# The mixes of odd heads on GpSimd in two passes, in the first prompt attention of a two-layer decoder step

## The reference

```python
s = jnp.einsum('bqhgcd,bkhcd->bhgcqk', q, k).astype(jnp.float32) * A_DH ** -0.5
...
p = jax.nn.softmax(jnp.where(mask, s + bias, -jnp.inf), axis=-1)
a = p[:, :, :, 0] - lam * p[:, :, :, 1]
o = jnp.einsum('bhgqk,bkhe->bqhge', a.astype(v.dtype), v)
```

## Time and profile before

| | us |
|---|---|
| median of 3 runs | 2816.69 |
| lowest and highest of them | 2816.53, 2825.95 |
| the profiled execution | 2817.39 |
| its span | 2815.7 |
| mean granted TensorE clock, share of full speed | 0.87 |

### The profile page before, as it was taken

How to read it: one execution, slowest core, us unless ns; L and a number is a source line. 1 busy time by engine, 2 the same in 40 slices (tenths; PEclk the granted TensorE clock), 3 DMA queues, 4 the chain that set the end, 5 groups by cost and what they waited for, 6 DMA issues and landing times. The chain is left out here.

```text
span 2815.7 us, 31305 instructions
## 1 busy us (share of the span) xinstructions
PE 2248.9 (80%) x9850; PEld 1356.4 (48%) x9850; DVE 1215.9 (43%) x2588; ACT 667.6 (24%) x1475; POOL 264.3 (9%) x410
## 2 busy tenths in 40 slices
PE   7999997986777775588845699975999938884688
PEld 3454565545676764356622344631654416661333
DVE  1000002675656553499821011064989946630111
ACT  2121001221222220366610011042012116640011
POOL 0000000002323220000013100031000000002300
PEclk9999999997887875699966799997999969986689
DMA  6001111100000002200029800111200120006841
GB/s 231 31 33 45 60 31 33 33 0 15 4 7 4 4 8 60 67 19 16 8 67 306 299 30 23 38 40 63 85 11 34 45 94 24 23 3 206 271 151 42
DMA packets 133268, 180.34 MB, mean 64 GB/s; under 512 B 23104, under 2 KB 103392, under 8 KB 132112
## 3 DMA queue, kind: packets, MB, share of 16 engines
q1 hardware_dynamic: 98648, 130.30, 13.9%
q10 hardware_dynamic: 24640, 25.41, 2.8%
q0 software_dynamic: 9856, 23.13, 2.5%
HBM read 152.48 MB, written 30.70 MB: 65 GB/s over the span
## 5 line engine op out<-in xcount | busy, mean ns | idle before, releaser
L538 PE MATMUL banks<-actT 128*128 128x350 f32 (+1 forms) x960 | 285.4, 461 | 12.3 <-ACTq L548 12.3
L198 PE MATMUL banks<-fr_w,actT 128*128 128x512 f32 (+1 forms) x640 | 238.9, 531 | 0.0
L538 PEld LDWEIGHTS banks<-actT 128*128 128x128 f32 x960 | 183.7, 192 | 113.1 <-ACTq L548 12.5
L474 PE MATMUL banks<-ptg_w,heads 128*128 128x512 f32 (+1 forms) x432 | 185.8, 592 | 1.7 <-ACT heads L426 1.7
L2726 DVE TENSOR_SCALAR_CACHE_REDUCE ch_hits<-c_chosen,ch_cand 128x384 bf16<-128x384 f32 (+1 forms) x186 | 175.8, 945 | 18.0 <-DVE ch_cand L2731 12.2
L198 PEld LDWEIGHTS banks<-fr_w,actT 128*128 128x128 f32 x640 | 113.8, 193 | 126.0 <-issue 126.0
L2170 PE MATMUL banks<-a_pages,actT 128*128 128x512 f32 x384 | 166.3, 593 | 0.0
L474 PEld LDWEIGHTS banks<-ptg_w,heads 128*128 128x128 f32 (+1 forms) x432 | 77.7, 180 | 109.3 <-issue 109.3
L600 PE MATMUL banks<-actT,aq_w 128*128 128x350 f32 (+1 forms) x384 | 120.1, 473 | 12.6 <-DMA aq_w<-w_in_e_dram 12.6
L1546 ACT ACTIVATE aa_prob<-aa_prob,aa_mx 128x128 f32<-128x128 f32 (+7 forms) x128 | 98.1, 767 | 74.0 <-DVE aa_mx L1647 73.7
L2170 PEld LDWEIGHTS banks<-a_pages,actT 128*128 128x128 f32 x384 | 72.3, 190 | 88.9 <-issue 88.9
(11 more groups left out here) (505 smaller groups left out, 3644.3 us busy)
## 6 DMA issues: line engine op xcount, KB each, us to landing
tok_rows<-fr_stage SPq DMA_DIRECT2D x8, 1028.0 KB, 3.9
fr_w<-w_in_e_dram SPq DMA_DIRECT2D x8, 1024.0 KB, 21.1
actT<-w_in_e_dram SPq DMA_DIRECT2D x6, 1024.0 KB, 5.3
a_pages<-cache_a_k_dram SPq DMA_DIRECT2D x48, 128.0 KB, 4.3
a_pages<-cache_a_v_dram SPq DMA_DIRECT2D x48, 128.0 KB, 4.0
a_pages<-w_out_e_dram SPq DMA_DIRECT2D x3, 2048.0 KB, 12.6
ptg_w<-w_in_o_dram SPq DMA_DIRECT2D x3, 2048.0 KB, 12.8
c_pages<-cache_c_k_dram SPq DMA_DIRECT2D x48, 128.0 KB, 3.9
```

Source lines behind the costliest of these rows:

```text
L198: last = nc.tensor.matmul(m.ps[:, j, 0:g[1]], m.actT[:, c, t * P:t * P + P], weights[j][:, c, :], start=(c == 0), stop=(c == KC - 1))
L474: last = nc.tensor.matmul(m.ps[0:r, j, 0:g[1]], rows[:, slot, c, 0:r], weights[j][:, c, :], start=(c == 0), stop=(c == KC - 1))
L538: last = nc.tensor.matmul(m.ps[:, NS * j + k, 0:tn], wring[:, s, c, j * P:(j + 1) * P], m.actT[:, c, t0:t0 + tn], start=(c == 0), stop=(c ...
```

## The change

For odd n the mix moves from DVE to POOL. POOL has no single instruction here for e0 + r e1, so it makes two: a TENSOR_SCALAR product of e1 with r into `mix`, and a TENSOR_TENSOR sum of `mix` and e0, in place. Between the two stands a wait on a new semaphore `mix_step`. The semaphore `combined` becomes `combined0` (signalled by DVE for even heads) and `combined1` (signalled by POOL for odd heads). DVE still computes reciprocal and ratio for all heads. The waits of `maxima` and of the transposes go to the semaphore of their parity. In POOL's program the new stage `mixed` has lag 1 and stands before `root`.

```diff
--- before.py
+++ after.py
@@ -1367,7 +1367,7 @@
             equal, rank = sb("equal", [P, wmax]), sb("rank", [P, wmax])
             neg, count, left = sb("neg", [P, 1]), sb("count", [P, len(tiles)]), sb("left", [P, len(tiles)])
         names = ("neg_set restored mark_step marked written bias_in bias_mm bias_out gate_in gain_in gain_out scores_mm near_out far_out lowest exp_half "
-                 "combined turned probs_out pv_mm o_out rs_out y_ready y_mm y_turned half_set step gated recip_out "
+                 "combined0 combined1 mix_step turned probs_out pv_mm o_out rs_out y_ready y_mm y_turned half_set step gated recip_out "
                  "ratio_out")
         s = {x: m.sem(f"{tag}_{x}") for x in names.split()}
 
@@ -1456,8 +1456,23 @@
                     pool.wait_ge(s["rs_out"], 2 * p.t + 1)
                     nc.gpsimd.tensor_tensor(rs[0:p.R], rs[0:p.R], minus_half[0:p.R], ALU.pow).then_inc(s["rs_out"], 1)
 
+                def mixed(n):
+
+                    p, h = heads[n]
+                    if n % 2 == 0:
+                        return
+                    out = mix[0:p.R, n % 2, 0:p.W]
+                    pool.wait_ge(s["ratio_out"], n + 1)
+                    if n >= 2:
+                        pool.wait_ge(s["turned"], groups_before[n - 1])
+                    nc.gpsimd.tensor_scalar(out, prob[0:p.R, n % 2, 1, 0:p.W], ratio[0:p.R, n % 2:n % 2 + 1], None,
+                                            ALU.mult).then_inc(s["mix_step"], 1)
+                    pool.wait_ge(s["mix_step"], n // 2 + 1)
+                    nc.gpsimd.tensor_tensor(out, out, prob[0:p.R, n % 2, 0, 0:p.W], ALU.add)\
+                        .then_inc(s["combined1"], 1)
+
                 if diff:
-                    pipeline(0, N, [(at_tile_end(root), TURN + 4)])
+                    pipeline(0, N, [(mixed, 1), (at_tile_end(root), TURN + 4)])
 
             @block.tensor
             def _(pe):
@@ -1492,7 +1507,7 @@
                 def turn(n, ks):
                     p, h = heads[n]
                     src = mix[:, n % 2] if diff else prob[:, n % 2, 0]
-                    pe.wait_ge(s["combined"] if diff else s["exp_half"], n + 1)
+                    pe.wait_ge(s[f"combined{n % 2}"] if diff else s["exp_half"], n // 2 + 1 if diff else n + 1)
                     for k in ks:
                         b0, bn = p.groups[k]
                         used = groups_before[n] + k + 1 - len(p.turns)
@@ -1612,7 +1627,7 @@
                     out = lambda c, w0, w1: prob[0:p.R, n % 2, c, w0:w1]
                     bias_p = bias[0:p.R, h, at:at + p.W - near]
                     if n >= 2 and diff:
-                        dve.wait_ge(s["combined"], n - 1)
+                        dve.wait_ge(s[f"combined{n % 2}"], n // 2)
                     elif n >= 2:
                         dve.wait_ge(s["turned"], groups_before[n - 1])
                     if not diff and p.t >= 2:
@@ -1662,12 +1677,14 @@
                     nc.vector.scalar_tensor_tensor(out=r, in0=inv[0:p.R, n % 4, 1:2], scalar=m.lam[0:p.R, 0:1],
                                                    in1=den[0:p.R, n % 4, 0:1], op0=ALU.mult, op1=ALU.mult)\
                         .then_inc(s["ratio_out"], 1)
+                    if n % 2:
+                        return
                     dve.wait_ge(s["ratio_out"], n + 1)
                     if n >= 2:
                         dve.wait_ge(s["turned"], groups_before[n - 1])
                     nc.vector.scalar_tensor_tensor(out=mix[0:p.R, n % 2, 0:p.W], in0=prob[0:p.R, n % 2, 1, 0:p.W],
                                                    scalar=r, in1=prob[0:p.R, n % 2, 0, 0:p.W], op0=ALU.mult,
-                                                   op1=ALU.add).then_inc(s["combined"], 1)
+                                                   op1=ALU.add).then_inc(s["combined0"], 1)
 
                 def gated(p):
                     R, w = p.R, (slice(0, p.R), p.t % 2)
```

## The result

The changed kernel takes 2902.96 us (median of 4 runs, 2901.01 to 2908.37) against 2817.25 us before, a ratio of 1.030 with a 95% interval of 1.0284 to 1.0317. It is slower by 86 us. The forecast was slower, 2865 us, with a range of 2848 to 2896. The sign held. The size was too small by 38 us, and the time lies 7 us above the range.

A forecast was written before the change was run, and what follows sets the result against it. The attention stage was taken as bound by DVE's program plus about 12 us of TensorE waits. 22.0 + 46.1 + 7.4 - 26.2 + 1.3 - 8 + 5 = 47.6 us over 2817.39 gave 2865, range 2848 to 2896.

The forecast's parts named there:

- What bounds the stage: First prompt attention: its length is DVE's program plus about 12 us of waits for TensorE.
- the question of DVE's pause: In attention, DVE stands still from an odd head's ratio to POOL's second pass end, 31 places, some 75 us.
- Term 1: Mixes of 32 odd heads removed from DVE: 26.2 us less.
- Term 2: POOL's first pass, the product with the ratio, priced from POOL's COPY: 22.0 us added.
- Rival (a): POOL's first pass costs as much as a two-input one, through its per-row value: 24 us more, 2889; chance 0.22.
- Term 3: POOL's second pass, the sum of two tiles, priced from TENSOR_TENSOR rows: 46.1 us added.
- Term 4: Hops between DVE and POOL and between POOL's steps, less two DVE hops that go: 7.4 us added.
- Term 5: At a tile's end DVE waits for POOL's power operation, queued behind an odd head's mix: 1.3 us added.
- Terms 6 and 7: DVE's waits for scores shrink during its pauses, 8 us back; TensorE's clock falls as it idles, 5 us added.

The follow-up runs named there:

- e2: The changed kernel with POOL making only the sum for odd heads, without the product with the ratio; 2839.8 us.
- e1b_copy: The changed kernel with POOL's first pass as a plain copy in place of the product with the ratio; 2859.97 us.
- e1_imm: The changed kernel with POOL's first pass multiplying by a constant (-0.25) in place of each row's ratio; 2898.7 us.
- e4: The changed kernel with TensorE computing the last chunk of scores of odd heads from the third on twice, filling its pauses; 2896.33 us.
- e5: Control: the kernel before, all mixes on DVE, with three slots of prob, four of mix and transposes one step later; 2820.18 us.
- e3_slots: The changed kernel with three slots of prob and four of the ratio in place of two; 2873.29 us.
- e6: The changed kernel with three slots of prob, four of mix and transposes one step later; 2840.79 us.
- e7: As e6, with POOL's power operation of a tile's end one step earlier in POOL's program; 2813.9 us, ratio 0.9983.
- e8: As e7, with POOL taking the mix of every fourth head only (16 of 64) and DVE the rest; 2817.77 us.

## Why the prediction was right or wrong

What bounds the stage, and **the question of DVE's pause**: right. DVE stands still in 31 places from the ratio to the end of POOL's sum, and e2 shows that a pass taken from POOL returns its whole time to the stage.

**Term 1**, the mixes removed from DVE: 26.2 us forecast, 26.2 us left on DVE for the even half.

**Term 2**, the first pass, is the step that failed. I chose the COPY as the nearest row "since the number of tiles read is the same", and put 22.0 us. It took 55.3 us, 33 us more. It even passed the upper bound of 46.1 us, since beside its 2.5 ns per column it has 0.29 us for each instruction, and my bound had taken none. e1b_copy shows that the copy's own price was right, and e1_imm that the form of the factor matters little. The right neighbour was the other arithmetic instruction, whatever its number of inputs. Rival (a) named this case at 2889 with 0.22. Its price was nearly right, but its reason, the value for each row, was not. With the term at 55.3, the forecast would have been 2898. The estimate from the page "GPSIMD Engine Reference" of the Trainium skill, section 3.1, was 1.5 ns per column for a loop at its best; the product measured 2.5, so that best case isn't reached by this instruction. Section 4.1 of the same page of the Trainium skill calls work with one input roughly line rate. The copy agrees, with 0.83 ns per column against 1.04 for DVE's mix, and the product does not.

**Term 3**, the second pass: 46.1 us forecast, 44.7 us measured, at 2.1 ns per column and 0.18 us. The estimate from section 3.1 of that page of the Trainium skill, which the sum had set aside, was 2.2 ns per column. As a slope it was nearer than the 2.5 of the rows; as a total, its 40.5 us were farther from 44.7 than the 46.1 of the rows, because it left no fixed time.

**Term 4**, the hops: 0.10 + 0.08 + 0.03 = 0.21 us, less the two of 0.07 us that go, makes 4.5 us for 32 heads, where I had 7.4. The step from one POOL instruction to the next is 0.08 us here, and was 0.18 in the rows I used.

**Term 5**, the wait for the power operation: 1.3 us forecast, none measured. In every tile but the last it took 1.67 us and not 2.57, so `normed` found it done. Only the last tile has such a wait, of 1.6 us, and it had one before.

**Terms 6 and 7**, 8 us given back and 5 us for the clock: the two together were -3 us and came to +1.4 us. The waits for scores went from 11.5 to 12.9 us. e4 shows the reason. At heads up to 256 columns they fell from 5.3 us before to 3.8. At the wider heads they were 6.2 us before, 9.1 with the change and 1.6 with the pauses filled. As an estimate from these, 1.5 + 4.6 = 6.1 us were given back, where I had 8, and the falling clock took 7.5 us, where I had 5. Their sum was wrong by 4 us.

The sum with the measured terms: 55.3 + 44.7 + 4.5 - 26.2 + 1.4 = 79.7 us. The stage grew by 79.0 us.

**Outside the stage** the span grew by 7.1 us, and I had expected nothing. 6.3 us of it lie in a loop of DVE in layer 1, the search for a threshold in 31 rounds, whose instructions the change doesn't touch. Its waits, before and after:

```profile
DVE ch_hits L2726 <- DVE ch_cand L2731: 12.2, 30, 0.4
```

```profile
DVE ch_hits L2743 <- DVE ch_cand L2748: 18.5, 30, 0.9
```

From first to last of its counting instructions the loop takes 293.0 us before and 293.1 us in e5, 299.3 us in the changed kernel, e1_imm, e1b_copy, e2_sum_only and e4_fill, 292.1 to 292.4 us in e3_slots, e6 and e7, and 295.8 us in e8. POOL's mixes don't decide it, since the loop is short in e3, e6 and e7, which have them too. That five kernels agree to 0.1 us speaks for something in the build, and the wait that differs is the one at the start of each round; what it is stays open, with one profile of each. The range should have allowed for some us of this kind.

The range failed through term 2: its upper end took rival (a) with only a little of the clock, and neither the fixed time of the pass nor a difference outside the stage. With term 2 right the forecast would have lain above that end, and without the 7.1 us outside the stage the time would have lain at it.

## What to carry to other kernels

Before moving work to an idle engine, look at what the busy engine does next: here its next instruction overwrote the input of the moved work, so the engine that was relieved stood still for the slower one. Extra slots moved that pause to the next in-order engine (e3), later consumers and an earlier place in POOL's queue removed it (e6, e7), and then the next bound was only 4 us away. When no row shows an instruction on an engine, price it by the nearest one that computes, not by a copy; here that would have left 9 us of the 33.

## What the runs showed of the hardware

A power operation over 128 x 8 values on POOL took 2.54 to 2.57 us when POOL had stood idle and 1.67 us right behind the sum of a mix, seven times out of seven in the changed kernel.

Some of POOL's and DVE's instructions that read SBUF got in each other's way, and not only for DVE. In e7 the product of 1024 columns took 3.75 us beside DVE's products of the tile's end, and 2.85 us alone:

```profile
1370.89 1.22 DVE L1700 TENSOR_TENSOR aa_y<-aa_o 128x1024 f32<-128x1024 f32 x1
1371.07 3.75 POOL L1469 TENSOR_SCALAR aa_mix<-aa_prob,aa_ratio 128x1024 f32<-128x1024 f32 x1 [4.61 <-DVE aa_ratio L1678]
...
1373.48 1.22 DVE L1705 TENSOR_TENSOR aa_y<-aa_o,aa_gate 128x1024 f32<-128x1024 f32 x1
...
1391.32 2.85 POOL L1469 TENSOR_SCALAR aa_mix<-aa_prob,aa_ratio 128x1024 f32<-128x1024 f32 x1 [2.67 <-DVE aa_ratio L1678]
```

The first and the third row shown are DVE's products over tiles of SBUF at a tile's end, the second is POOL's product beside them, and the last is such a product beside none. Another product of 3.75 us in that stretch, at 1382.46, stood beside `normed`, and one beside DVE's maxima, which read PSUM, took 2.85 us. Both long products began while a product of DVE was running. The third row began in the middle of POOL's product and took its usual 1.22 us, so not every overlap costs; which ones do stays open. In the changed kernel nothing of this appeared, since DVE always stood still while POOL worked.
